# Linear attention: the inter-chunk products load their states from copies laid out slot by slot

## The chip, the cores and the metric

One NeuronCore of a Trainium2 chip. The time is the device time of the kernel in microseconds (us), the median of three runs; a profiled execution of the same program gives the rows of the trace.

## The reference, cut to what matters

The program is two two-layer networks, one after the other, in float32. The change touches the second network alone, in whose layers one of three mixers is a gated linear attention over 512 latent and 256 context tokens, with 6 heads, keys of 32 and values of 64, in both directions:

```python
GLA_HEADS, GLA_DK, GLA_DV, GLA_CHUNK = 6, 32, 64, 16

def gla_chunked(q, k, v, g, s0):
    ...
    b = jnp.cumsum(g, axis=2)
    b_last = b[:, :, -1:]
    q_dec = q * jnp.exp(b)
    k_inv = k * jnp.exp(-b)
    k_end = k * jnp.exp(b_last - b)
    ...
    a = jnp.einsum('bnihk,bnjhk->bnhij', q_dec, k_inv)
    a = jnp.where(causal, a, 0.0)
    o_intra = jnp.einsum('bnhij,bnjhv->bnihv', a, v)

    def step(s, xs):
        qd, ke, vv, dec = xs
        o = jnp.einsum('bihk,bhkv->bihv', qd, s)
        s = s * dec[..., None] + jnp.einsum('bjhk,bjhv->bhkv', ke, vv)
        return s, o
    ...
    s_final, o_inter = lax.scan(step, s0, xs)
    o = o_intra + jnp.moveaxis(o_inter, 0, 1)
```

Each chunk of 16 tokens takes the state left by the chunks before it (48 chunks in all: 16 of the context, 32 latent), and its output is the product within the chunk plus the decayed queries times that state. Both directions are added, normalized by head and multiplied with a gate.

## The kernel before, in words

Everything is written by hand for the five engines, with semaphores. In each of the two layers `gated_linear` first computes the decays and then calls `gla_group` twice, once for each group of three heads (96 partitions: 3 heads x 32 key rows). The calls are the four groups spoken of below. The first layer puts out all six token tiles of 128 (`upd` = 6), the second layer only the four latent ones (`upd` = 4).

In a group, TensorE makes each tile's state updates (L3111) and transposed scores (L3102); ScalarE, and VectorE for a sixth of them, place the updates in the tile `states`, `ST[partition, direction, 64 value columns, 49 slots]`: for each value column the 49 slots lie side by side, so that a chunk's state, 64 values, is read with a step of 49 words. VectorE masks the scores into `scoresT`. Then VectorE turns updates into states with four scans (L3190), each along the slots of all its rows: two for each direction, over 24 and over 40 of the 64 value columns, with decays that ScalarE has widened (L3216). Beside them TensorE runs the products within the chunks (L3122, scores x values, all six or four tiles), which read the scores, and then the inter-chunk products (L3128): for each tile and chunk the stationary operand is the chunk's state, 96 x 64, the moving one the chunk's queries, 96 x 48. All tiles of the first direction come first, behind the second scan; then the second direction, behind the fourth scan, tile by tile, each tile followed by the transposes (L3138) of the one before. A float32 product is two passes on TensorE, each with its own weight load.

Behind the products ScalarE copies a tile out (L3249), TensorE turns it, VectorE and ScalarE normalize it and VectorE multiplies it with the gate; the gate's activation (L3231) is ScalarE's, its multiplication with a gain (L3090) GpSimd's. In the first group of a layer TensorE at the end also turns the queries and keys of the next group (L3155). Before all this GpSimd has widened values (L3059) and copied queries (L3066).

Of the kernel before, what the change touches and what calls it, by code (L numbers as in the profile page):

```python
# [46 lines left out]
GLA_H, GLA_DK, GLA_DV, GLA_LR, CHUNK, GLA_TAU = 6, 32, 64, 16, 16, 16.0  # L47
QK = GLA_H * GLA_DK
GV = GLA_H * GLA_DV
NCH = (T + TC) // CHUNK  # L50
# [72 lines left out]
class ModulationEnd:  # L123
# [26 lines left out]
    def copy(self, dve, turned, out):  # L150
        dve.wait_ge(turned, 1)
        dve.tensor_copy(self.rows, self.bank).then_inc(out, 1)
# [13 lines left out]
class Program:  # L166
# [2841 lines left out]
    def gla_group(self, layer, grp, UG, UR, KE, DEC, MX, ON, QB, QT, KT, gain, ms, eps_t, upd, slot, SL, following):  # L3008
# [8 lines left out]
        NC8, W3, N = P // CHUNK, HG * GLA_DK, NTT * HG  # L3017
# [3 lines left out]
        V = lambda t, hh: UG[:, t, 2 * QK + (grp * HG + hh) * GLA_DV:2 * QK + (grp * HG + hh + 1) * GLA_DV]  # L3021
        with ExitStack() as ctx:
            ST = self.sbuf(ctx, "states", [W3, 2, GLA_DV, SL])
# [3 lines left out]
                sem(n) for n in ("updates", "up_out_v", "up_out_a", "zeroed", "blocked", "scanned", "scored", "masked",  # L3027
                                 "mixed", "out_done", "turned", "rows_done"))
            widened, blocked_back = sem("widened"), sem("blocked_back")
            spare = MX[:, 0:3, :].rearrange("p k n -> p (k n)")  # L3030
            VX = spare[:, 0:VR * NC8 * GLA_DV].rearrange("p (r c v) -> p r c v", r=VR, v=GLA_DV)
            parts = [(0, 24), (24, GLA_DV)]
            DX = [self.sbuf(ctx, "decay_wide", [W3, 24, SL])[:, :, :],
                  spare[0:W3, 0:(GLA_DV - 24) * SL].rearrange("p (v s) -> p v s", s=SL)]
            AT = self.sbuf(ctx, "scoresT", [P, upd, HG, 2, P])
            OT = spare[0:GLA_DV, 0:2 * HG * P].rearrange("p (r h n) -> p r h n", r=2, h=HG)
            SQ = spare[:, 2 * HG * P:2 * HG * P + 2 * W].rearrange("p (r n) -> p r n", r=2)
            own = slice(grp * W, (grp + 1) * W)
# [24 lines left out]
            def block_q(copy, d, hh):  # L3063

                r = slice(hh * GLA_DK, (hh + 1) * GLA_DK)
                return copy(QB[r, d, :, hh, :], QT[r, d, :].rearrange("p (c n) -> p c n", n=CHUNK))  # L3066

            def place(copy, n, d):

                t, hh = n // HG, n % HG  # L3070
                s0 = slot(d, t * NC8) + 1
                r = slice(hh * GLA_DK, (hh + 1) * GLA_DK)
                dst = ST[r, 0, :, s0:s0 + NC8] if d == 0 else ST[r, 1, :, s0 - NC8 + 1:s0 + 1][:, :, ::-1]
                return copy(dst, UB(n)[d * GLA_DK:(d + 1) * GLA_DK].rearrange("p (c v) -> p v c", v=GLA_DV))

            with nc.Block() as block:
                @block.gpsimd
                def _(pool):
                    for t in range(NTT):
                        for n in range(t * HG, (t + 1) * HG):  # L3080
                            if from_pool(n):
                                expand(pool, n)
                        if t % 2 == 1:
                            pool.wait_ge(expanded[0], expands((t + 1) * HG - 2))
                            block_q(pool.tensor_copy, 0, t // 2).then_inc(blocked, 1)
                            pool.wait_ge(blocked, t // 2 + 1)
                    pool.wait_ge(gate_silu, 1)
                    rows = UR[:, 0:upd, own].rearrange("p t (h v) -> p t h v", v=GLA_DV)
                    for t in range(upd):
                        pool.tensor_tensor(rows[:, t], rows[:, t], gain[:, :].unsqueeze(1).broadcast_to(  # L3090
                            [P, HG, GLA_DV]), ALU.mult).then_inc(gate_ready, 1)

                @block.tensor
                def _(pe):
# [24 lines left out]
                    for t in range(upd):  # L3119
                        for hh in range(HG):  # L3120
                            for d in range(2):
                                pe.matmul(OB(t)[:, hh, :], V(t, hh), AT[:, t, hh, d, :],  # L3122
                                          start=(hh == 0 and d == 0), stop=False, skip_group_check=True)
                    pe.wait_ge(blocked, HG)

                    def inter(t, d):
                        for c in range(NC8):
                            ins_ = pe.matmul(OB(t)[:, :, c * CHUNK:(c + 1) * CHUNK], ST[:, d, :, slot(d, t * NC8 + c)],  # L3128
                                             QB[:, d, t * NC8 + c], start=False, stop=(d == 1 and c == NC8 - 1),
                                             skip_group_check=True)  # L3130
                        return ins_
# [7 lines left out]
                                                ident[0:GLA_DV, 0:GLA_DV])  # L3139
                        ins_.then_inc(turned, 1)  # L3140

                    pe.wait_ge(scanned, 2)
                    for t in range(upd):
                        inter(t, 0)
                    pe.wait_ge(scanned, 4)
                    pe.wait_ge(blocked_back, HG)
                    for t in range(upd):
                        inter(t, 1).then_inc(mixed, 1)
# [64 lines left out]
                def _(act):  # L3213
                    def widen(k):
                        a, b = parts[k % 2]
                        act.copy(DX[k % 2], DEC[:, k // 2, grp, :].unsqueeze(1).broadcast_to([W3, b - a, SL])).then_inc(  # L3216
                            widened, 1)
# [10 lines left out]
                    for k in (2, 3):  # L3228
                        act.wait_ge(scanned, k - 1)
                        widen(k)  # L3230
                    act.activation(UR[:, 0:upd, own], UR[:, 0:upd, own], ACT.Silu).then_inc(gate_silu, 1)  # L3231

                    def square(t):
                        act.wait_ge(rows_done, t + 1)
# [325 lines left out]
```

## Time and profile before

| | |
|---|---|
| median of 3 runs | 3917.28 us (3915.54 to 3919.32) |
| profiled execution | 3916.27 us |
| its span | 3914.5 us |
| mean granted TensorE clock | 0.918 |
| TensorE busy | 3387.8 us (87%) |
| VectorE busy | 2694.3 us (69%) |
| ScalarE busy | 2125.3 us (54%) |
| GpSimd busy | 572.5 us (15%) |

The four groups stand at about 2147 to 2214, 2214 to 2277, 3312 to 3368 and 3368 to 3423 us of the span, with a granted TensorE clock of 0.76, 0.74, 0.74 and 0.75. Times in rows count from the span's start; PE is TensorE's matmul, PEld its weight load, DVE VectorE, ACT ScalarE, POOL GpSimd. PEclk is the granted clock as a share of 2.4 GHz.

### The profile page before, as it was taken

The page shows a single profiled execution, that of the slowest core. Times are in us where ns is not written, and L with a number is a line of the kernel's source. Part 1 is how long each engine was busy: PE and PEld are TensorE (multiplying, and loading weights), DVE is VectorE, ACT ScalarE, POOL GpSimd, SP SyncE. Part 2 cuts the span into 40 slices and gives each one's busy share as a digit, 9 for nine tenths or more (in the row PEclk, how much of TensorE's full clock was granted, in tenths as well). Part 3 has the DMA queues.
Part 4 walks back from the last instruction along what each step waited for, and adds up shares of the span by engine and source line. Part 5 has one row for each costly group of instructions (what it writes and reads, how often), then busy time and mean ns, then how long its engine had stood idle before and what let it go on. Part 6 is the DMA issues. An engine that isn't in the chain of part 4 may idle for free. (4 is left out here: it accounts for less than half of the span.)

```text
span 3914.5 us, 50754 instructions
## 1 busy us (share of the span) xinstructions
PE 3387.8 (87%) x17144; PEld 2769.9 (71%) x17144; DVE 2694.3 (69%) x3836; ACT 2125.3 (54%) x2780; POOL 572.5 (15%) x286
## 2 busy tenths in 40 slices
PE   8869999957978999948888987999997888879997
PEld 6757777746766777737777676888776777568875
DVE  3669999966668999976865656774565555555545
ACT  3539999943538999953444623332234445634433
POOL 0005333410004334420020300000000011300000
PEclk9879999978979999978989888999998989789998
DMA  3149999942048999953320032331331210022222
GB/s 111 49 152 396 419 418 410 407 180 94 12 164 356 419 416 416 412 200 117 104 70 2 1 108 100 117 117 65 113 105 50 58 61 1 3 80 96 93 84 81
DMA packets 148091, 651.33 MB, mean 166 GB/s; under 512 B 23478, under 2 KB 36968, under 8 KB 89448
## 3 DMA queue, kind: packets, MB, share of 16 engines
q1 hardware_dynamic: 137576, 631.59, 42.6%
q0 software_dynamic: 10080, 16.80, 1.1%
q8 instruction: 84, 1.38, 0.1%
q10 hardware_dynamic: 288, 1.05, 0.1%
q14 instruction: 63, 0.52, 0.0%
HBM read 645.01 MB, written 24.26 MB: 171 GB/s over the span
## 5 line engine op out<-in xcount | busy, mean ns | idle before, releaser
L1762 DVE TENSOR_TENSOR w_low<-w_raw,w_high 128x2048 fp32r<-128x2048 f32 x392 | 881.9, 2282 | 55.5 <-ACT w_high L1759 51.2
L1759 ACT CAST w_high<-w_raw 128x2048 fp32r<-128x2048 f32 x392 | 746.1, 1910 | 77.5 <-DMA w_raw<-in_moe_gate_dram 33.8
L2069 PE MATMUL banks<-w_high,x_split 128*128 128x512 f32 x1024 | 421.0, 411 | 46.6 <-DVE w_low L1762 39.1
L2069 PE MATMUL banks<-w_low,x_split 128*128 128x512 f32 x1024 | 407.8, 398 | 0.0
L529 PE MATMUL banks<-w_high,x_high 128*128 128x512 f32 (+2 forms) x808 | 309.6, 383 | 57.4 <-DVE w_low L435 31.5
L399 ACT CAST w_high<-w_raw 128x512 fp32r<-128x512 f32 (+2 forms) x200 | 117.8, 589 | 427.1 <-PE banks L529 421.2
L3376 PE MATMUL banks<-x_high,w_high 128*128 128x512 f32 (+1 forms) x1056 | 320.9, 358 | 21.2 <-DVE w_low L3414 21.2
L3376 PE MATMUL banks<-x_high,w_low 128*128 128x512 f32 (+1 forms) x1056 | 324.0, 361 | 0.0
L3376 PE MATMUL banks<-x_low,w_high 128*128 128x512 f32 (+1 forms) x1056 | 320.1, 357 | 0.0
L529 PE MATMUL banks<-w_high,x_low 128*128 128x512 f32 (+2 forms) x808 | 300.3, 372 | 0.0
L529 PE MATMUL banks<-w_low,x_high 128*128 128x512 f32 (+2 forms) x808 | 300.3, 372 | 0.0
L2069 PEld LDWEIGHTS banks<-w_high,x_split 128*128 128x128 f32 x1024 | 193.9, 189 | 126.4 <-DVE w_low L1762 81.9
L2019 POOL DMA_INDIRECT expert_rows<-ys,sidx x34 | 258.9, 7615 | 120.5 <-ACT ys L2239 119.6
L3399 ACT ACTIVATE convolved<-banks,taps 128x768 f32<-128x768 f32 (+1 forms) x88 | 78.0, 886 | 312.4 <-PE banks L3376 312.3
L785 PE MATMUL banks<-w_high,x_high 128*128 128x512 f32 (+2 forms) x516 | 207.4, 402 | 35.8 <-DVE w_low L753 18.9
L529 PEld LDWEIGHTS banks<-w_high,x_high 128*128 128x128 f32 x808 | 154.1, 191 | 102.0 <-DVE w_low L435 49.6
L2069 PEld LDWEIGHTS banks<-w_low,x_split 128*128 128x128 f32 x1024 | 194.2, 190 | 41.0
L3376 PEld LDWEIGHTS banks<-x_high,w_high 128*128 128x128 f32 x1056 | 176.3, 189 | 54.4 <-issue 21.8
L785 PE MATMUL banks<-w_low,x_high 128*128 128x512 f32 (+2 forms) x516 | 202.3, 392 | 0.0
L785 PE MATMUL banks<-w_high,x_low 128*128 128x512 f32 (+2 forms) x516 | 202.2, 392 | 0.0
L433 DVE TENSOR_TENSOR x_low<-mixT,x_high 128x768 fp32r<-128x768 f32 x112 | 107.3, 958 | 136.2 <-ACT x_high L400 135.7
L3376 PEld LDWEIGHTS banks<-x_high,w_low 128*128 128x128 f32 x1056 | 175.1, 189 | 30.7
(410 smaller groups left out, 7241.4 us busy)
## 6 DMA issues: line engine op xcount, KB each, us to landing
w_raw<-in_moe_gate_dram SPq DMA_DIRECT2D x132, 1024.0 KB, 10.5
w_raw<-in_moe_up_dram SPq DMA_DIRECT2D x132, 1024.0 KB, 10.2
w_raw<-in_moe_down_dram SPq DMA_DIRECT2D x132, 1024.0 KB, 10.9
w_raw<-in_ffn_w_up_dram SPq DMA_DIRECT2D x44, 1024.0 KB, 4.9
w_raw<-in_ffn_w_down_dram SPq DMA_DIRECT2D x88, 256.0 KB, 2.7
modulation<-in_w_adaT_dram SPq DMA_DIRECT2D x42, 512.0 KB, 4.2
hiddenT<-in_w_adaT_dram SPq DMA_DIRECT2D x28, 512.0 KB, 3.7
w_raw<-in_w_cols_dram SPq DMA_DIRECT2D x48, 256.0 KB, 2.9
```

Of the source, the lines that this page charges most:

```text
L399: act.copy(WS[0][:, rest % S, 0:w], W[:, rest, 0:w])
L433: dve.tensor_tensor(XS[1][:, rest % S, :], x_tile(k), XS[0][:, rest % S, :].bitcast(F32), ALU.subtract)
L529: ins_ = pe.matmul(psum_of(g), st[:, rest % S, a:b], mv[:, rest % S, x:y], start=start and first + second == 0, stop=stop and first == 1)
L785: ins_ = pe.matmul(psum_of(g), XS[first][:, k, t * P:(t + 1) * P], WS[second][:, u % S, 0:w], start=(i == 0 and first + second == 0), stop ...
L1759: act.copy(ex["WS"][0][:, v % HIGH, :], ex["WR"][:, v % RAW, :]).then_inc(ex["high"], 1)
L1762: dve.tensor_tensor(ex["WS"][1][:, v % LOW, :], ex["WR"][:, v % RAW, :], ex["WS"][0][:, v % HIGH, :].bitcast(F32), ALU.subtract).then_inc( ...
L2019: pool.indirect_dma_start(out=Y, out_offset=bass.IndirectOffsetOnAxis(ap=sidx[:, 0:1], axis=0), in_=YS[:, :], in_offset=None, bounds_check ...
L2069: ins_ = pe.matmul(GU[b][m], stationary(b, kk), WS[w][:, s, k * BANK:(k + 1) * BANK], start=(kk == 0 and w == 0), stop=(kk == KD - 1 and w ...
L3376: ins_ = pe.matmul(U(b, ab)[:, x:y], WS[first][b][:, at:at + P], XS[second][:, k, x:y], start=(k == 0 and first + second == 0), stop=(k == ...
L3399: act.activation(Z[:, ab, :], U(b, ab)[:, 0:ntok], ACT.Identity, bias=cv[:, bass.ds(f * 8 + (4 * ab + 3), 1)], scale=cv[:, bass.ds(f * 8 + ...
```

## The change

The scanned states are copied so that a slot's 64 values lie side by side, and L3128's successor loads the copies. The first direction's copy is put over the scores, whose place is free once the products within the chunks are through, and the second direction's over the rows of `states` that held the first direction. GpSimd copies value columns 0 to 24 and 48 to 64 of each direction, ScalarE columns 24 to 48. New semaphores order this: `within` is raised by the last product within the chunks, `slotted_by_pool` by each of GpSimd's four copies and `slotted_by_act` by ScalarE's two. TensorE waits for two and one of them ahead of the first direction, for four and two ahead of the second, in place of the scans.

```diff
+            within, slotted_p, slotted_a = sem("within"), sem("slotted_by_pool"), sem("slotted_by_act")
...
+            by_slot = [x[:, 0:NCH * GLA_DV].rearrange("p (s v) -> p s v", v=GLA_DV) for x in (
+                AT[0:W3].rearrange("p t h d n -> p (t h d n)"), ST[:, 0].rearrange("p v s -> p (v s)"))]
+            own_rows, late_rows = (24, 48), [(0, 24), (48, GLA_DV)]
...
+            def by_slots(copy, d, rows):
+
+                a, b = rows
+                return copy(by_slot[d][:, :, a:b], ST[:, d, a:b, 0:NCH].rearrange("p v s -> p s v"))
...
+                    pool.wait_ge(within, 1)
+                    for k in range(4):
+                        pool.wait_ge(scanned, k + 1)
+                        if k == 2:
+                            pool.wait_ge(slotted_a, 1)
+                        by_slots(pool.tensor_copy, k // 2, late_rows[k % 2]).then_inc(slotted_p, 1)
+                        pool.wait_ge(slotted_p, k + 1)
                     pool.wait_ge(gate_silu, 1)
...
-                                pe.matmul(OB(t)[:, hh, :], V(t, hh), AT[:, t, hh, d, :],
-                                          start=(hh == 0 and d == 0), stop=False, skip_group_check=True)
+                                ins_ = pe.matmul(OB(t)[:, hh, :], V(t, hh), AT[:, t, hh, d, :],
+                                                 start=(hh == 0 and d == 0), stop=False, skip_group_check=True)
+                    ins_.then_inc(within, 1)
...
-                            ins_ = pe.matmul(OB(t)[:, :, c * CHUNK:(c + 1) * CHUNK], ST[:, d, :, slot(d, t * NC8 + c)],
+                            ins_ = pe.matmul(OB(t)[:, :, c * CHUNK:(c + 1) * CHUNK], by_slot[d][:, slot(d, t * NC8 + c)],
...
-                    pe.wait_ge(scanned, 2)
+                    pe.wait_ge(slotted_p, 2)
+                    pe.wait_ge(slotted_a, 1)
                     for t in range(upd):
                         inter(t, 0)
-                    pe.wait_ge(scanned, 4)
+                    pe.wait_ge(slotted_p, 4)
+                    pe.wait_ge(slotted_a, 2)
...
+                    act.wait_ge(within, 1)
+                    by_slots(act.copy, 0, own_rows).then_inc(slotted_a, 1)
                     act.activation(UR[:, 0:upd, own], UR[:, 0:upd, own], ACT.Silu).then_inc(gate_silu, 1)
+                    act.wait_ge(scanned, 4)
+                    act.wait_ge(slotted_p, 2)
+                    act.wait_ge(slotted_a, 1)
+                    by_slots(act.copy, 1, own_rows).then_inc(slotted_a, 1)
```

GpSimd's queue in the first layer's first group, from its last copy of queries to the group's end, before (`u_r` is the gate, `q_blocks` the blocked queries):

```order
L3059 TENSOR_TENSOR mixT<-u_gla,consts 128x512 x4
L3066 COPY q_blocks<-q_decT 32x48x16
L3090 TENSOR_TENSOR u_r<-u_r,gain 128x192 x6
L3076 UNCONDITIONAL_BRANCH
L183 ISA
```

and now:

```order
L3063 TENSOR_TENSOR mixT<-u_gla,consts 128x512 x4
L3070 COPY q_blocks<-q_decT 32x48x16
L3075 COPY scoresT<-states 96x48x24
L3075 COPY scoresT<-states 96x48x16
L3075 COPY states<-states 96x48x24
L3075 COPY states<-states 96x48x16
L3106 TENSOR_TENSOR u_r<-u_r,gain 128x192 x6
```

Four copies now stand between the queries and the gate. On TensorE, at the same place, the products within the chunks and the first ones behind them, before (the last dimensions, 3x16, are a chunk's 48 query columns):

```order
L3122 MATMUL banks<-scoresT,u_gla 64x128 x36
L3128 MATMUL banks<-q_blocks,states 64x3x16 x64
L3138 MATMUL banks<-consts,mixT 128x64 x3
L3128 MATMUL banks<-q_blocks,states 64x3x16 x8
L3138 MATMUL banks<-consts,mixT 128x64 x3
```

and now:

```order
L3138 MATMUL banks<-scoresT,u_gla 64x128 x36
L3145 MATMUL banks<-q_blocks,scoresT 64x3x16 x48
L3145 MATMUL banks<-q_blocks,states 64x3x16 x16
L3155 MATMUL banks<-consts,mixT 128x64 x3
L3145 MATMUL banks<-q_blocks,states 64x3x16 x8
```

The number and the order of TensorE's products are as before; the first 48 read what now lies in the scores' place, the rest the slots over the first direction's rows. ScalarE gets one copy ahead of the gate's activation and one behind it.

## Rows read from the trace of the kernel before

**Rows 1.** Timeline of the first group: start, us, engine, line, operation, names, shapes, count.
```profile
2173.28 8.05 PE L3122 MATMUL banks<-scoresT,u_gla 128*64 128x128 f32 x72 [1.24 <-DVE scoresT L3181]
...
2175.81 4.21 DVE L3190 TENSOR_TENSOR_SCAN states<-mixT,states 96x1960 f32<-96x1960 f32 x1
...
2179.94 2.58 DVE L3190 TENSOR_TENSOR_SCAN states<-decay_wide,states 96x1176 f32<-96x1176 f32 x1
...
2181.16 14.40 PE L3128 MATMUL banks<-q_blocks,states 96*64 96x48 f32 x128
...
2182.44 4.21 DVE L3190 TENSOR_TENSOR_SCAN states<-mixT,states 96x1960 f32<-96x1960 f32 x1
...
2184.51 5.28 POOL L3090 TENSOR_TENSOR u_r<-u_r,gain 128x192 f32<-128x192 f32 x6 [14.88 <-ACT u_r L3231]
```

**Rows 2.** L3128 alone in two stretches: us, PE, PEld busy (count), PEclk, DMA.
```profile
2181.50:2185.00 3.50, 3.50 (x34) 3.50 (x33) 1.00 0.02 5
2186.00:2193.00 7.00, 7.00 (x65) 7.00 (x65) 0.50 0.00 0
```

**Rows 3.** Two stretches: PE, PEld, DVE, ACT, POOL busy (count), PEclk, DMA.
```profile
2185.40:2209.00 23.60, 23.60 (x185) 21.97 (x185) 8.26 (x24) 6.71 (x16) 4.38 (x6) 0.50 0.00 1
2209.40:2212.00 2.60, 1.26 (x12) 1.00 (x10) 2.06 (x7) 2.50 (x10) 0.00 (x0) 1.00 0.00 0
```

**Rows 4.** L1463 (a product elsewhere) alone in two stretches, columns as in rows 2.
```profile
246.50:249.90 3.40, 3.40 (x32) 3.40 (x32) 1.00 0.02 5
250.30:256.60 6.30, 6.30 (x31) 6.30 (x31) 0.50 0.00 0
```

**Rows 5.** Timeline of TensorE in the same two stretches.
```profile
246.44 3.76 PE L1463 MATMUL banks<-ring,hT 128*128 128x36 f32 x32 [1.02 <-ACT hT L1288]
...
250.01 6.81 PE L1463 MATMUL banks<-ring,hT 128*128 128x36 f32 x31
```

**Rows 6.** Timeline of the third and the fourth group: scans and products.
```profile
3339.76 4.21 DVE L3190 TENSOR_TENSOR_SCAN states<-mixT,states 96x1960 f32<-96x1960 f32 x1
...
3343.90 2.58 DVE L3190 TENSOR_TENSOR_SCAN states<-decay_wide,states 96x1176 f32<-96x1176 f32 x1
...
3344.12 10.91 PE L3128 MATMUL banks<-q_blocks,states 96*64 96x48 f32 x96 [1.57 <-DVE states L3190]
...
3399.28 2.58 DVE L3190 TENSOR_TENSOR_SCAN states<-decay_wide,states 96x1176 f32<-96x1176 f32 x1
...
3399.50 10.92 PE L3128 MATMUL banks<-q_blocks,states 96*64 96x48 f32 x96
```

**Rows 7.** L3090: timeline of the first one, and all 20 (ns min/median/max).
```profile
2184.51 2.53 POOL L3090 TENSOR_TENSOR u_r<-u_r,gain 128x192 f32<-128x192 f32 x1 [14.88 <-ACT u_r L3231]
...
L3090 POOL TENSOR_TENSOR u_r<-u_r,gain x20: 581/586/2851, 2184.5 to 3407.4; 128x192 f32<-128x192 f32 x20
```

**Rows 8.** Timeline of GpSimd and VectorE at two places ahead of the products.
```profile
2161.26 0.92 DVE L3059 TENSOR_TENSOR mixT<-u_gla,consts 128x512 f32<-128x512 f32 x1 [0.81 <-PE banks L3111]
2161.70 1.16 POOL L3066 COPY q_blocks<-q_decT 32x768 f32<-32x768 f32 x1
...
2218.91 1.04 POOL L3059 TENSOR_TENSOR mixT<-u_gla,consts 128x512 f32<-128x512 f32 x1 [0.67 <-PE banks L3111]
...
2220.01 0.81 POOL L3066 COPY q_blocks<-q_decT 32x768 f32<-32x768 f32 x1
...
2220.12 1.25 DVE L3059 TENSOR_TENSOR mixT<-u_gla,consts 128x512 f32<-128x512 f32 x1 [2.29 <-PE banks L3111]
```

**Rows 9.** Durations by line: ns min/median/max, first and last start, shapes.
```profile
L3128 PE MATMUL banks<-q_blocks,states x640: 208/311/348, 2181.2 to 3415.0; 96*64 96x48 f32 x160
...
L1463 PE MATMUL banks<-ring,hT x128: 271/279/409, 246.4 to 1153.2; 128*128 128x36 f32 x128
...
L3066 POOL COPY q_blocks<-q_decT x12: 599/951/1163, 2153.7 to 3388.0; 32x768 f32<-32x768 f32 x6, 32x512 f32<-32x512 f32 x6
...
L3216 ACT COPY decay_wide<-decay x8: 1174/1178/1181, 2147.8 to 3396.1; 96x1176 f32<-96x1176 f32 x8
```

## The prediction

> **What bounds the stage now.** I read the timeline of the linear attention's four groups first, since the change touches nothing else: two head groups in the first layer (products for six token tiles), two in the second (four tiles). In the first group [rows 1] TensorE is the bound from the score products on: L3122 starts as soon as the scores are masked and ends at 2181.33 (2173.28 + 8.05), the inter-chunk products of L3128 follow at 2181.16 without a gap, and TensorE then has no pause that an engine elsewhere explains until the group's end. VectorE's four scans run back to back beside it: the second, with which the first direction is complete, ends at 2180.02, before TensorE gets there; the fourth ends at 2186.65, while the first direction's products still run. So the scans cost nothing today. The third group differs a little: there L3122 is through early and TensorE waits 1.57 us for its second scan [rows 6].
>
> A product of L3128 is two passes, each with a weight load of 64 columns and 48 moving columns. 128 passes take 14.40 us, the last of them 0.31: 111 ns from start to start [rows 1, 9]. That is the price at both clock levels: 34 passes in 3.50 us at a granted 1.00 (2.4 GHz), 65 in 7.00 us at 0.50 (1.2 GHz) [rows 2]. A pass that does not care about TensorE's clock is held by the reading of its weights, which lie 49 words apart in the states' rows. The products spend most of their time at the low level: the clock falls at 2185.4, after some 4 us of these thin products, and stays at 0.50 for 23.6 us, until the 128-column transposes of the group's end [rows 3].
>
> **The weight load, slot by slot.** After the change the 64 columns lie side by side. The nearest rows for that are L1463's: 128 columns side by side, 36 moving columns, so the load bounds them too. Less the last one's own 0.28 and 0.41 us, 32 passes take 3.76 us, 112 ns from start to start, at 1.00, and 31 passes 6.81 us, 213 ns, at 0.50 [rows 4, 5, 9]. This load does follow the clock. Half the columns make 56 ns at the high level and 107 ns at the low one. The gain per pass is therefore 55 ns at 1.00 and 4 ns at 0.50, and all of it for 640 passes is 35.2 us or 2.6 us. Everything turns on the clock during the products.
>
> **The new wait.** The first direction's copies go into the scores' place, so none can start before L3122 is through. ScalarE copies a third of it; GpSimd two parts, one after the other, of 24 and 16 rows (1152 and 768 elements for a partition). TensorE now waits for both. VectorE's scans are running at just that time, and the rows show what GpSimd does beside VectorE. The first multiplication of L3090 takes 2.53 us when it falls into the fourth scan, its kind 0.586 [rows 7]: subtracting, it began in effect at 2186.45, 0.20 us before the scan's recorded end of 2186.65. It holds for a copy as well: L3066's copy takes 1.16 us when a two-input operation of VectorE is running, 0.81 when none is, and in that last row VectorE is the one that waits: its 0.92 us become 1.25, so that it began 0.37 us before GpSimd's recorded end [rows 8]. The two take turns, whole instruction by whole instruction.
>
> The Trainium skill says the same more widely (SBUF — State Buffer, Who interferes with whom): VectorE and GpSimd share a pair of SBUF ports as an exclusive lock, held for the whole instruction, also against a VectorE operation with two SBUF inputs. The scans are of that kind, so by this rule every copy during them waits; were it not so, the time would be the last rival's below.
>
> So in the first group: the third scan ends at 2182.52 and GpSimd's copy of a us runs from 2182.32. The fourth scan has been queued since 2182.44, while GpSimd must first see its own semaphore, so I let the scan go next: from 2181.95 + a, for 4.21 less the 0.08 by which scans overlap in the record, to 2186.08 + a. The second copy, of b us, runs from 2185.88 + a, and with 0.15 us for the semaphore (the same as between the third group's second scan, which ends at 3343.97, and its first product at 3344.12 [rows 6]) TensorE starts at 2186.03 + a + b instead of 2181.16: later by 4.87 + a + b. The second group repeats these rows one for one, so it has the same. The same working gives 5.87 + a + b for the fourth (its third scan ends at 3401.86, its products start at 3399.50 [rows 6]), and 1.73 + a + b for the third, where the first copy goes behind the second scan and only the short third scan (2.58 us) lies between the copies.
>
> Price of a and b: no row shows a GpSimd copy that reads at this stride. From below, L3066's copies, 0.81 us for 768 elements and 0.60 for 512 [rows 8, 9], make 0.83 ns for an element: a = 1.13, b = 0.81. From above, L3059's 1.04 us for 512 elements, 2.0 ns for each [rows 8]: a = 2.3, b = 1.55. The copy is nearest to L3066; the stride doubled a weight load (111 against 56 ns), and I put half of that on it: a = 1.6, b = 1.1. The waits then are 7.57, 7.57, 4.43 and 8.57 us, together 28.1 us, between 25.1 and 32.7.
>
> **The clock after that.** TensorE stands still for 7 us where it now works, and then runs products of the same 48 columns every 107 ns, hardly denser than those that stay at 0.50 for 23.6 us now. The clock fell after thinner work and rose only with wide transposes. I take 0.50 for all 640 passes: 2.6 us saved.
>
> The Trainium skill gives a rule without the clock (TensorE: Matmul & The Clock Gate, LDWEIGHTS): a load takes its columns over 1.2 ns, here 53 ns at either level. By it all passes would cost about 56 and save 35.2 us, 3912 in the second rival below; but 128 columns took 213 ns at 0.50, not 107, so the measurement decides against it.
>
> **The rest costs nothing.** ScalarE's first copy (1.17 us for 1176 elements side by side [rows 9], twice that at worst) lies beside GpSimd's; it pushes the gate's activation back, for which only GpSimd's multiplications wait, and the second copy is done some 1.5 to 3 us after the fourth scan, near 2190. GpSimd's two copies for the second direction end near 2191.6 in the first group, and its six multiplications 3.5 us later. All this lies beside the first direction's products (48 products, 96 passes, 10.3 us from 2188.7; in the third group 6.9 us to 3355.4, the copies being ready at 3355.0). If this cover went, the third group would lose up to 2.8 us, as the rivals count. The scans' lateness of some 1.2 us matters to nobody: VectorE's next work is a tile's rows, after the second direction's first products. Nothing is queued behind TensorE's new wait but its own products. The transfers are untouched.
>
> **Sum.** 28.1 - 2.6 = +25.5 us on the profiled execution's own 3916.27 us (span 3914.5): 3941.8. The runs' median lies 1.0 higher, so 3942 stands between. Its own range: 25.1 - 2.6 to 32.7, that is 3938 to 3950; it also holds the case that the change doesn't make loads any quicker (28.1, 3944).
>
> **Rivals.**
> 1. GpSimd's second copy slips in behind the first, before the fourth scan. For it: the copies are adjacent in its queue. Against: the scan already waits for the port, GpSimd for a semaphore. The starts then slip by 4.2, 4.2, 2.7 and 5.2 us, 16.2 in all, and the third group's second direction, whose copies now wait behind the fourth scan, costs 2 us: +15.6, 3932.
> 2. The clock is high during the products. For it: at 1.00, passes of 56 ns are twice as dense as now, so once high it may stay. Against: it must rise first, after a pause, from 107 ns passes. At 1.00 throughout: 28.1 - 35.2 + 2.8 (the third group's second direction then waits for GpSimd's fourth copy) = -4.3, 3912. If it rises after the first 64 passes of each group, 4 x 64 x 51 ns = 13 us are lost again: 3924. I price it at 3918.
> 3. Faster: the scans do not hold the copies. Then TensorE waits only for a + b and three semaphores after L3122: 3.3, 3.3, 1.6 and 3.2 us. With the clock kept, 11.4 - 35.2 + 3.9 (third and fourth group waiting for the fourth scan and ScalarE's copy) = -19.9: 3896. It decides where the pause stays so short that the clock holds; with the low clock it is 11.4 - 2.6, 3925. For it: no row has a copy beside a scan. Against: [rows 7, 8].
>
> **Chances.** The forecast 0.69 (with the loads that don't gain), rival 1 0.08, rival 2 0.13, rival 3 0.06, dearer copies beyond 3950 0.04. A change of under 0.2% (7.8 us) is about what a measurement of this kernel can't tell from none: 3909.4 to 3925.1. Faster by more: rival 3 with its clock and a little of rival 2, 0.07. Within: rival 2, 0.14. Slower: 0.79. The range 3920 to 3950 holds the forecast, rival 1 and the upper third of rival 2.
>
> **What would show it.** Right: a pause of TensorE of 4 to 9 us ahead of the first inter-chunk product in each group; in GpSimd's first copy about 1 us of waiting and in its second some 4 us, ending just behind the fourth scan (the third in the third group); that scan recorded a good 1 us longer; passes of 107 ns at 0.50. Wrong: passes near 56 ns with a granted 1.00, copies that end inside a scan, or a pause under 4 us in the six-tile groups.

## The result, and the profile after

The changed kernel takes 3950.26 us (median of six runs, 3937.55 to 3954.91), the kernel before 3917.57 us beside it: a ratio of 1.0084, 95% interval 1.0070 to 1.0098. The change costs 32.7 us. The profiled execution took 3949.64 us with a span of 3947.9; its mean granted TensorE clock was 0.913, against 0.918 before.

This is the first group in the timeline after the change (start, us, engine, line; L3138 are the products within the chunks, L3145 the inter-chunk ones, L3209 the scans, L3075 the new copies, L3106 the multiplications with the gain).

```profile
2172.38 8.05 PE L3138 MATMUL banks<-scoresT,u_gla 128*64 128x128 f32 x72 [1.24 <-DVE scoresT L3200]
...
2179.04 2.58 DVE L3209 TENSOR_TENSOR_SCAN states<-decay_wide,states 96x1176 f32<-96x1176 f32 x1
...
2180.55 8.47 POOL L3075 COPY scoresT<-states 96x1152 f32<-96x1152 f32 x2 [11.82 <-PE banks L3138]
2180.89 2.26 ACT L3075 COPY scoresT<-states 96x1152 f32<-96x1152 f32 x1
2181.54 6.21 DVE L3209 TENSOR_TENSOR_SCAN states<-mixT,states 96x1960 f32<-96x1960 f32 x1
...
2189.08 3.79 POOL L3075 COPY states<-states 96x1152 f32<-96x1152 f32 x2
...
2189.10 2.25 ACT L3075 COPY states<-states 96x1152 f32<-96x1152 f32 x1 [3.47 <-issue]
2189.12 10.45 PE L3145 MATMUL banks<-q_blocks,scoresT 96*64 96x48 f32 x96 [8.70 <-POOL scoresT L3075]
2192.96 3.33 POOL L3106 TENSOR_TENSOR u_r<-u_r,gain 128x192 f32<-128x192 f32 x6
```

In [rows 1] the inter-chunk products followed the products within the chunks without a gap. Now TensorE waits 8.70 us, and the timeline names GpSimd's copy as what it waited for. GpSimd's two copies take 8.47 us while the scans run and 3.79 us, with the same shapes, when they don't. The fourth scan is recorded 2.00 us longer than before (6.21 against 4.21). ScalarE's copy takes 2.26 us beside a scan and 2.25 without one: nothing holds it.

The copies one by one, from the line's own view in the stretch of the first direction and in that of the second (ns min/median/max; with two instructions these are the shorter and the longer).

```profile
L3075 POOL COPY scoresT<-states x2: 3106/4206/5307, 2180.5 to 2183.7; 96x1152 f32<-96x1152 f32 x1, 96x768 f32<-96x768 f32 x1
...
L3075 POOL COPY states<-states x2: 1492/1866/2239, 2189.1 to 2191.4; 96x1152 f32<-96x1152 f32 x1, 96x768 f32<-96x768 f32 x1
```

Undisturbed the copies cost a = 2.24 and b = 1.49 us. In the first direction they are recorded with 3.11 and 5.31: the first waits about 0.87 us for the third scan to end, the second about 3.82 us for the fourth.

The stretches of the first group (busy time of PE, PEld, DVE, ACT, POOL, then PEclk), to be read beside [rows 2, 3]:

```profile
2180.40:2184.40 4.00, 0.03 (x1) 0.00 (x0) 4.00 (x2) 3.98 (x3) 3.79 (x2) 0.99 0.00 0
2184.40:2189.10 4.70, 0.00 (x0) 0.01 (x1) 3.36 (x1) 1.22 (x2) 4.64 (x2) 0.50 0.00 0
2189.10:2212.20 23.10, 23.08 (x204) 22.27 (x204) 3.99 (x13) 7.80 (x14) 7.04 (x8) 0.50 0.01 1
```

TensorE's clock falls to 0.50 in the pause, and all inter-chunk products run at that level. The 96 passes of the first direction take 10.45 us, 107 ns from start to start.

In the kernel before, the products within the chunks took 5.42 us in the third group and 7.09 in the fourth:

```profile
3337.13 5.42 PE L3122 MATMUL banks<-scoresT,u_gla 128*64 128x128 f32 x48 [2.42 <-issue]
...
3392.50 7.09 PE L3122 MATMUL banks<-scoresT,u_gla 128*64 128x128 f32 x48 [2.42 <-issue]
```

Now they take 7.09 us in the third group as well:

```profile
3354.41 7.09 PE L3138 MATMUL banks<-scoresT,u_gla 128*64 128x128 f32 x48 [2.41 <-issue]
...
3361.17 2.58 DVE L3209 TENSOR_TENSOR_SCAN states<-decay_wide,states 96x1176 f32<-96x1176 f32 x1
...
3361.62 9.53 POOL L3075 COPY scoresT<-states 96x1152 f32<-96x1152 f32 x2 [10.78 <-PE banks L3138]
```

The window over the third group's products has a mean granted clock of 0.76:

```profile
3354.40:3361.40 7.00, 6.99 (x48) 6.85 (x48) 6.88 (x3) 4.80 (x6) 0.00 (x0) 0.76 0.01 2
```

So the first copy comes 0.45 us after the third scan has begun, and the first inter-chunk product starts 16.74 us after the group's first scan, as in the other three groups.

### The profile page after: what moved, and what is told of

It reads as the page before. It is cut to its first block and busy times, and to the rows that moved or that the text cites. A ratio compares the mean times of both kernels' runs of the same rounds, so it can differ in the third digit from the quotient of the medians.

```text
span 3947.9 us, 50798 instructions
## 1 busy us (share of the span) xinstructions
PE 3387.1 (86%) x17144; PEld 2770.1 (70%) x17144; DVE 2700.6 (68%) x3836; ACT 2141.6 (54%) x2788; POOL 638.5 (16%) x302
## 5 line engine op out<-in xcount | busy, mean ns | idle before, releaser
L3401 PEld LDWEIGHTS banks<-x_low,w_high 128*128 128x128 f32 x1056 | 174.5, 189 | 30.7
## 6 DMA issues: line engine op xcount, KB each, us to landing
w_raw<-in_moe_gate_dram SPq DMA_DIRECT2D x132, 1024.0 KB, 10.5
```

Source lines behind the costliest of these rows:

```text
L3401: ins_ = pe.matmul(U(b, ab)[:, x:y], WS[first][b][:, at:at + P], XS[second][:, k, x:y], start=(k == 0 and first + second == 0), stop=(k == ...
```

## The experiments

The timeline gives a measure of the stage: the start of the first and of the last inter-chunk pass, counted from the start of the group's first scan. The third column adds up what the last pass has moved in all four groups against the kernel before. Stretches outside the stage differ by some us from run to run (the first group's first scan starts between 2172.0 and 2176.7 us), so medians and stage agree within 4 us only. The measure ends with the last pass: in no_copies, whose last pass in the first group comes 10.5 us earlier, the second group's first scan comes 8.2 us sooner.

| kernel | first / last pass, us: first group; third; fourth | stage, sum | median, us | ratio, 95% interval |
|---|---|---|---|---|
| before | 7.88 / 31.80; 6.88 / 22.41; 6.88 / 22.41 | 0 | 3917.6 to 3918.2 | |
| changed | 16.74 / 39.81; 16.74 / 31.64; 16.74 / 31.64 | +34.5 | 3950.26 | 1.0084 (1.0070 to 1.0098) |
| hold_fourth | 12.92 / 35.99; 12.91 / 29.64; 12.62 / 29.35 | +22.6 | 3944.78 | 1.0065 (1.0052 to 1.0078) |
| one_copy | 12.69 / 35.76; 12.69 / 28.52; 12.68 / 28.52 | +20.1 | 3937.44 | 1.0055 (1.0042 to 1.0068) |
| turned_loops | 16.49 / 39.56; 16.49 / 31.39; 16.49 / 31.39 | +33.5 | 3948.08 | 1.0078 (1.0066 to 1.0091) |
| plain_copies | 14.99 / 38.07; 14.98 / 29.88; 10.85 / 25.75 | +23.3 | 3938.65 | 1.0056 (1.0043 to 1.0070) |
| no_copies | 7.88 / 21.26; 6.88 / 21.52; 6.88 / 21.52 | -22.9 | 3895.68 | 0.9943 (0.9931 to 0.9956) |
| filled | 12.66 / 28.69; 13.80 / 25.82; 12.66 / 25.08 | -0.5 | 3918.07 | 1.0002 (0.9993 to 1.0011) |
| second_only | 7.87 / 31.33; 6.88 / 25.09; 6.88 / 25.10 | +4.4 | 3925.07 | 1.0016 (1.0007 to 1.0025) |
| early | 8.48 / 28.16; 6.88 / 22.41; 6.88 / 22.41 | -7.3 | 3907.73 | 0.9978 (0.9969 to 0.9987) |
| early_filled | 8.50 / 24.52; 6.88 / 22.38; 6.88 / 22.39 | -14.4 | 3906.49 | 0.9975 (0.9965 to 0.9984) |

The second group repeats the first within 0.05 us, but for the last pass of filled (28.29) and early_filled (24.78).

### hold_fourth: is it the scans that hold the copies?

```diff
                         dve.wait_ge(widened, k + 1)
+                        if k == 3:
+                            dve.wait_ge(slotted_p, 2)
```

> The changed kernel, with one wait more: VectorE's fourth scan starts only when GpSimd has made both of its first-direction copies. My theory (GpSimd's copies and VectorE's scans take turns, so the second copy is held behind the whole fourth scan): the second copy follows the first at once and takes about 1.5 us; TensorE's pause ahead of the first inter-chunk product falls from 8.7 and 9.8 us to about 4.9 and 6.0; in the two four-tile groups the late fourth scan and the copies behind it cost about 1.3 us each ahead of the second direction; 3950 - 15 + 2.6 = about 3938. Rival (the copies are slow by themselves, the scans don't hold them): the second copy still takes about 5 us, and the pause stays or grows: 3950 or more.

The timeline of its first group, and of the copies and scans of its fourth:

```profile
2184.55 4.66 POOL L3075 COPY scoresT<-states 96x1152 f32<-96x1152 f32 x2 [11.82 <-PE banks L3138]
...
2189.28 2.21 POOL L3075 COPY states<-states 96x1152 f32<-96x1152 f32 x1
...
2189.32 10.45 PE L3145 MATMUL banks<-q_blocks,scoresT 96*64 96x48 f32 x96 [4.88 <-POOL scoresT L3075]
2189.32 6.28 DVE L3211 TENSOR_TENSOR_SCAN states<-mixT,states 96x1960 f32<-96x1960 f32 x1 [3.69 <-POOL scoresT L3075]
...
3417.40 5.43 PE L3138 MATMUL banks<-scoresT,u_gla 128*64 128x128 f32 x48 [2.42 <-issue]
...
3422.95 7.08 POOL L3075 COPY scoresT<-states 96x1152 f32<-96x1152 f32 x2 [9.11 <-PE banks L3138]
3424.17 4.58 DVE L3211 TENSOR_TENSOR_SCAN states<-decay_wide,states 96x1176 f32<-96x1176 f32 x1
```

With the scan out of the way both copies together take 4.66 us instead of 8.47, and the pause is 4.88 us, as expected (4.9): the turns are shown. What I had not expected is the next turn: GpSimd, now free, starts its third copy (2.21 us) 0.04 us ahead of the fourth scan, which is recorded 2.07 us longer for it. The late states cost the second direction of the four-tile groups 1.8 us each, not 1.3. The stage gains 11.9 us on the changed kernel, the medians 5.5 only: 3944.78 us where 3938 was expected, and the intervals of the two ratios overlap. It is the trace that shows the turn here, not the time.

The fourth group shows something else. Here the products within the chunks took 5.43 us, the first copy was ready before the second scan ended, and the third scan is the one recorded 2.00 us longer (4.58 against 2.58): the copy got in ahead of it. I come back to this below.

### one_copy: one turn instead of two

```diff
-            own_rows, late_rows = (24, 48), [(0, 24), (48, GLA_DV)]
+            own_rows, late_rows = (0, 24), (24, GLA_DV)
...
-                    for k in range(4):
-                        pool.wait_ge(scanned, k + 1)
+                    for k in range(2):
+                        pool.wait_ge(scanned, 2 * k + 2)
...
```

> The changed kernel, with GpSimd's two copies of a direction made into one: rows 24 to 64 in one instruction once both scans of that direction are done; ScalarE copies rows 0 to 24. My theory (each separate copy loses a turn to a scan): one copy of 1920 elements takes about 3.7 us once it has its turn, and loses only the turn to the third scan: pause of about 4.9 us in the six-tile groups and 6.0 in the four-tile ones, about 3938, the same as with the fourth scan held back. Rival (the copies' elements set the time, not turns): the pause stays at 8.7 to 9.8 us, about 3950.

Timeline of its first group:

```profile
2182.52 4.42 POOL L3075 COPY scoresT<-states 96x1920 f32<-96x1920 f32 x1 [11.82 <-PE banks L3138]
...
2183.51 7.53 DVE L3209 TENSOR_TENSOR_SCAN states<-mixT,states 96x1960 f32<-96x1960 f32 x1
...
2187.04 10.44 PE L3145 MATMUL banks<-q_blocks,scoresT 96*64 96x48 f32 x96 [4.64 <-POOL scoresT L3075]
```

The same 1920 elements in one instruction are through after one turn: a pause of 4.64 us, and 3937.44 us where 3938 was expected. (In the four-tile groups of this run the products within the chunks ended early, so the pause from there is 7.4 us, while the first product still starts 12.69 us after the first scan.) The fourth scan waits 3.3 us, and nobody waits for it long: the second direction of a four-tile group starts 0.9 us late.

### turned_loops and plain_copies: what a copy costs

```diff
-                return copy(by_slot[d][:, :, a:b], ST[:, d, a:b, 0:NCH].rearrange("p v s -> p s v"))
+                return copy(by_slot[d][:, :, a:b].rearrange("p s v -> p v s"), ST[:, d, a:b, 0:NCH])
```

> The changed kernel, with the two loops inside every copy exchanged: it reads 48 slots side by side and writes them 64 words apart, the same elements to the same places. Theory that the jumping reads doubled the price: GpSimd's copies fall from 2.25 and 1.48 us to about 1.13 and 0.81, ScalarE's from 2.26 to about 1.2; the pause is 1.8 us shorter in each of the four groups, about 3943. Rival (jumping writes cost the same as jumping reads, or the price goes by element whatever the order): 2.25 and 1.48 us again, 3950.

```diff
+                by_row = by_slot[d].rearrange("p s v -> p (s v)")[:, a * NCH:b * NCH].rearrange("p (v s) -> p v s", s=NCH)
+                return copy(by_row, ST[:, d, a:b, 0:NCH])
```

> The changed kernel, whose copies move the same rows to the same buffers without turning them: row after row, 48 words side by side on both sides. The products load the same addresses as in the changed kernel and so multiply wrongly ordered numbers. Theory that jumping by many words, on the reading or on the writing side, doubles the price of an element: GpSimd's copies fall to about 1.13 and 0.81 us, ScalarE's to about 1.2 us, the pause in each group is 1.8 us shorter, about 3943. Rival (this many elements over 96 partitions cost that much in any order): 2.25 and 1.48 us as before, 3950.

First the copies of the second direction, undisturbed, in turned_loops, from the line's view:

```profile
L3075 POOL COPY states<-states x2: 1491/1832/2173, 2189.6 to 2191.9; 96x1152 f32<-96x1152 f32 x1, 96x768 f32<-96x768 f32 x1
...
L3075 ACT COPY states<-states x1: 2173/2173/2173, 2189.7 to 2189.7; 96x1152 f32<-96x1152 f32 x1
```

The same in plain_copies:

```profile
L3076 POOL COPY states<-states x2: 822/983/1144, 2189.6 to 2190.8; 96x1152 f32<-96x1152 f32 x1, 96x768 f32<-96x768 f32 x1
...
L3076 ACT COPY states<-states x1: 1152/1152/1152, 2189.6 to 2189.6; 96x1152 f32<-96x1152 f32 x1
```

Jumping on the writing side costs as much as jumping on the reading side (2.17 and 1.49 us), so the rival of turned_loops was right; without jumps GpSimd needs 1.14 and 0.82 us, ScalarE 1.15. So a turned copy costs twice a plain one, on both engines. The first product of plain_copies starts 1.75 us earlier (14.99 against 16.74).

Its fourth group ran with early products within the chunks, as the fourth of hold_fourth, and here nothing is held back by hand:

```profile
3413.66 5.43 PE L3139 MATMUL banks<-scoresT,u_gla 128*64 128x128 f32 x48 [2.42 <-issue]
...
3419.21 5.32 POOL L3076 COPY scoresT<-states 96x1152 f32<-96x1152 f32 x2 [9.12 <-PE banks L3139]
3420.43 3.48 DVE L3210 TENSOR_TENSOR_SCAN states<-decay_wide,states 96x1176 f32<-96x1176 f32 x1
...
3423.83 4.79 DVE L3210 TENSOR_TENSOR_SCAN states<-mixT,states 96x1960 f32<-96x1960 f32 x1
```

The window over its products within the chunks:

```profile
3413.60:3419.00 5.40, 5.34 (x48) 5.21 (x48) 5.23 (x2) 4.74 (x5) 0.00 (x0) 1.00 0.02 3
```

At a clock of 1.00 TensorE was done with them after 5.43 us, the first copy went behind the second scan and the second behind the third, and the first product started at 10.85 instead of 14.98 us: 4.1 us less, for nothing but the order of the turns. That is why plain_copies came to 3938.65 where 3943 was expected.

### no_copies: what the contiguous loads are worth

```diff
-                        by_slots(pool.tensor_copy, k // 2, late_rows[k % 2]).then_inc(slotted_p, 1)
...
-                    by_slots(act.copy, 0, own_rows).then_inc(slotted_a, 1)
...
-                    pe.wait_ge(slotted_p, 2)
-                    pe.wait_ge(slotted_a, 1)
+                    pe.wait_ge(scanned, 2)
...
```

> The changed kernel without the copies: the inter-chunk products load 64 words side by side out of the scans' own tile, so they multiply wrong numbers, and TensorE waits for the scans as before the change. This is what the contiguous loads are worth without the pause. My theory (a load that follows the clock, and denser passes without a pause hold the high level): passes of 56 ns at a granted 1.00; 640 x 55 ns = 35 us less, and 3 us given back in each of the four-tile groups to the fourth scan: about 3888. Rival (the clock falls for passes of 48 columns anyway): 107 ns at 0.50 for most of them, about 3915.

Stretches of the first and of the third group:

```profile
2183.40:2197.00 13.60, 13.23 (x207) 12.62 (x204) 8.03 (x10) 7.70 (x13) 5.27 (x6) 1.00 0.01 2
3338.50:3346.80 8.30, 8.26 (x70) 7.83 (x70) 0.97 (x3) 3.05 (x6) 2.01 (x4) 0.50 0.01 2
```

In the six-tile groups, where the products follow without a pause, the clock stays at 1.00 to their end: the first direction's 96 passes start within 5.52 us, 58 ns apart, and the last pass comes 10.5 us earlier. In the four-tile groups, which start with the wait of 1.57 us that stands in [rows 6] too and wait again for the fourth scan, it falls to 0.50, and 0.9 us is all that is gained. Both theories were right, each in one kind of group, which gives 3896, between their 3888 and 3915.

### filled: is it the pause that takes the clock?

```diff
+                    def fill(n):
+                        for _ in range(n):
+                            pe.matmul(self.ps[0:GLA_DV, 7, 0:P], ident[:, 0:GLA_DV], masks[:, 0, :], start=True, stop=True)
...
+                    fill(20 if upd == NTT else 32)
                     pe.wait_ge(slotted_p, 1)
                     pe.wait_ge(slotted_a, 1)
...
+                    fill(9 if upd == NTT else 17)
                     pe.wait_ge(slotted_p, 2)
...
```

> The version with one GpSimd copy per direction, whose TensorE pauses are filled with products of constants of 128 moving columns into a spare bank (20 and 9 of them in the six-tile groups, 32 and 17 in the four-tile ones, ahead of the first and of the second direction). They are extra work whose results nobody reads. My theory (the pause is what drops TensorE's clock, and with it goes the worth of the contiguous loads): TensorE stays at a granted 1.00, passes take 57 to 60 ns as without copies, the last inter-chunk product comes about 7.5 us earlier in the six-tile groups and 3 us earlier in the four-tile ones than with one copy: 3937 - 20 = about 3917. Rival (the clock falls for other reasons, the pause has no part in it): passes of 107 ns, 3937 or a little more.

The filling (L3145) and the first direction (L3149) in the first group's timeline:

```profile
2179.89 4.53 PE L3145 MATMUL banks<-consts 128*64 128x128 f32 x40
...
2184.68 5.80 PE L3149 MATMUL banks<-q_blocks,scoresT 96*64 96x48 f32 x96 [0.26 <-POOL scoresT L3075]
```

Stretches of the first direction and of the start of the second, first group:

```profile
2184.60:2190.50 5.90, 5.82 (x98) 5.83 (x99) 4.12 (x1) 2.40 (x2) 1.68 (x2) 1.00 0.00 0
2192.40:2199.00 6.60, 6.29 (x90) 5.74 (x89) 1.26 (x5) 4.08 (x8) 3.35 (x7) 1.00 0.00 0
```

The copies, the turns and the late start are those of one_copy (first product at 12.66 us), but with TensorE kept busy the clock stays at 1.00, in the first group until 0.9 us ahead of the last pass, and the passes take 59 ns. That alone is worth 19.4 us: 3918.07 against 3937.44, with 3917 expected. (In the third group, whose products within the chunks took 7.09 us, the filling ends later than the copies, and the first product starts at 13.80.) With the clock kept, this version costs nothing against the kernel before.

### second_only: the half that is hidden

```diff
-                    for k in range(4):
+                    for k in range(2, 4):
...
-                    by_slots(act.copy, 0, own_rows).then_inc(slotted_a, 1)
...
-                            ins_ = pe.matmul(OB(t)[:, :, c * CHUNK:(c + 1) * CHUNK], by_slot[d][:, slot(d, t * NC8 + c)],
+                            ins_ = pe.matmul(OB(t)[:, :, c * CHUNK:(c + 1) * CHUNK], (by_slot[1][:, slot(d, t * NC8 + c)] if d else ST[:, 0, :, slot(d, t * NC8 + c)]),
...
```

> Half of the change: only the second direction's states are copied (into the scores' place), the first direction's products load the scanned rows as before the change. My theory (the loss is the wait ahead of the first direction; copies that lie beside its products cost nothing, and at the low clock the contiguous loads give back 4 ns a pass): no pause ahead of the first product, nothing lost in the six-tile groups, a wait of about 3 us ahead of the second direction in each four-tile group, where only 7 us of products cover the fourth scan and the copies: 3918 - 2 + 6 = about 3922. Rival (the copies cost wherever they are, by slowing scans, products or gate work): about half of the change's 33 us or more, 3934 and up.

The first group's timeline:

```profile
2183.23 10.83 PE L3143 MATMUL banks<-q_blocks,states 96*64 96x48 f32 x96
...
2184.75 7.61 POOL L3075 COPY scoresT<-states 96x1152 f32<-96x1152 f32 x2 [13.05 <-DVE states L3206]
```

Again GpSimd's copy sits behind the fourth scan, now for 3.8 us, and in the six-tile groups nobody minds: the last pass is 0.5 us earlier than before the change. In the four-tile groups the second direction starts 3.0 us later, as expected. By the stage this makes +4.4 us; the median is 7.4 us up. Most of the change's loss, 30 of 34.5 us by the stage and 25 of 32.7 by the medians, is the first direction's.

### early and early_filled: the copies where they fit

The first layer only; the second is as before the change. The place of the queries and keys is free from the first scan on, so the copies need not wait for the products within the chunks, and ScalarE and VectorE make them.

```diff
+                        by_slots(act.copy, 0, (0, 24)).then_inc(slotted_a, 1)
+                        act.wait_ge(scanned, 2)
+                        by_slots(act.copy, 0, (24, 40)).then_inc(slotted_a, 1)
+                        widen(3)
...
+                            by_slots(dve.tensor_copy, d, (40, GLA_DV)).then_inc(slotted_v, 1)
...
+                        pe.wait_ge(slotted_v, 1)
+                        pe.wait_ge(slotted_a, 2)
...
```

> First layer only (the second layer's groups are as before the change): the copies of the first direction go into the place of the decayed queries and keys, which is free before the within-chunk products end, and are made by ScalarE (rows 0 to 40, the first 24 while the second scan runs) and VectorE (rows 40 to 64, between its second and third scan); GpSimd builds the second direction's query blocks instead of ScalarE. My theory (the loss is the wait and the clock that falls in it): TensorE's pause ahead of the first inter-chunk product is under 1 us, the clock holds through the first direction, 57 ns a pass; the second direction waits some 2.5 us for the later scans and their copies. If the clock holds through that as well, the last product comes 7 to 8 us earlier than before the change in each of the two groups, about 3903; if it falls there, 2 us earlier, about 3913. Rival (a strided copy on VectorE costs several us, or copies and scans disturb each other on these engines too): a pause of 3 us or more, the clock falls, 3920 to 3930.

> The early copies, with 12 products of constants on TensorE ahead of the second direction, whose results nobody reads. My theory (a pause drops the clock): if the plain early version loses its clock between the directions, this one keeps it, with passes of 57 to 60 ns to the end: about 3903. Rival (the clock falls during the thin passes themselves, whatever stands between them): the same time as the plain early version.

The timeline of early's first group:

```profile
2183.48 1.57 ACT L3076 COPY qk_turned<-states 96x768 f32<-96x768 f32 x1 [0.78 <-DVE states L3212]
2183.48 1.20 DVE L3076 COPY qk_turned<-states 96x1152 f32<-96x1152 f32 x1
...
2185.19 5.77 PE L3142 MATMUL banks<-q_blocks,qk_turned 96*64 96x48 f32 x96 [0.44 <-ACT qk_turned L3076]
```

Two of its stretches, the first direction and the start of the second:

```profile
2185.20:2191.00 5.80, 5.76 (x96) 5.64 (x96) 5.80 (x2) 5.77 (x4) 1.60 (x1) 1.00 0.01 3
2193.00:2199.00 6.00, 6.00 (x59) 5.59 (x60) 0.78 (x3) 1.80 (x5) 2.40 (x5) 0.60 0.01 3
```

The two directions in early_filled:

```profile
2180.70:2186.50 5.80, 5.80 (x98) 5.80 (x99) 5.80 (x2) 5.77 (x4) 1.60 (x1) 1.00 0.01 3
2188.90:2196.90 8.00, 7.63 (x110) 6.99 (x108) 2.48 (x8) 4.50 (x10) 2.02 (x4) 1.00 0.01 2
```

The pause ahead of the first direction is 0.44 us and the clock holds. Ahead of the second direction TensorE waits 2.03 us, and the clock falls behind that wait in early, not in early_filled: the last pass comes 3.6 us earlier than before the change in the one, 7.3 in the other. Both kernels are faster than either of the two compared: 0.9978 and 0.9975. Expected were about 3903 where the clock holds to the end and 3913 where it falls between the directions. The two profiled executions took 3901.58 (early_filled) and 3911.67 (early), but the medians lie between, 3906.49 and 3907.73: that early_filled beats early, as the stage says by 7 us, they do not confirm. The mean granted clocks of the executions overlap, 0.920 to 0.923 and 0.918 to 0.921, so the two traces show what the filling does in one execution each, not how often early loses its clock.

## Why the prediction was right, and where it was wrong

It said 3942 with a range up to 3950, and slower; it is slower, and at 3950.26 just past the range. By its own steps:

- **TensorE's new wait, its place and its cause**: right. The pause stands ahead of the first inter-chunk product in each group, and GpSimd's second copy ends behind the fourth scan (in the third group too, where the third was predicted; see below). That copies and scans take turns by whole instructions is shown by hold_fourth and one_copy, which remove a turn each and move the first product by 3.8 and 4.1 us in a six-tile group. The Trainium skill's rule (SBUF — State Buffer, Who interferes with whom), an exclusive lock held for the whole instruction, agrees; it also says that ScalarE waits for nobody, as its 2.26 us beside a scan against 2.25 show.
- **The clock and the passes**: right. 0.50 for all inter-chunk products, 107 ns a pass; the time from the first to the last pass fell from 23.92 to 23.07 and from 15.53 to 14.90 us, 2.96 us in all against the 2.6 predicted. The high level's price, 56 ns, was measured as 58 to 59 (no_copies, filled). Rival 2 needed the clock high: its passes came, 59 ns at 1.00, only where the pause is filled, short or absent (filled, early, the six-tile groups of no_copies).
- **The hidden work**: right. The second direction follows the first without a pause in the changed kernel.
- **The step that failed: the size of the delays**, 28.1 us predicted and 37.4 measured (8.86 us in each six-tile group, 9.86 in each four-tile one). Three terms make up the 9.3 us.
  1. The price of a and b. The prediction put half of the stride's doubling on L3066's price, 1.6 and 1.1 us; the doubling was whole, 2.24 and 1.49 (plain_copies gives 1.14 and 0.82 without it, which is the prediction's lower bound). That is 1.03 us in each group, 4.1 us.
  2. The order of turns in the third group. The prediction let its first copy go behind the second scan, which the run before allowed, with its products within the chunks through in 5.42 us; in the profiled run after they ran at a mean clock of 0.76, took 7.09 us and ended behind the third scan's start, and the group lost the turn: 4.1 us. What the prediction took for a property of the third group differs from execution to execution: early, whose second layer works as in the kernel before, has 7.09 us in the third group and 5.43 in the fourth. The mechanism as predicted does occur, when the products end early: hold_fourth's fourth group has its first product 5.74 us later than before where the prediction's 1.73 + a + b gives 5.46 with the measured a and b, and plain_copies shows both orders in one run.
  3. The hand-over. The fourth scan began 0.11 us ahead of the copy's recorded end, not 0.37, and took its whole 4.21 us, not 4.13; the second copy and TensorE followed 0.07 us sooner than reckoned. Net, that is 0.26 us in each group, 1.0 us.
- **The sum**: 37.43 - 2.96 = +34.47 us in the stage; the profiled executions differ by 33.4, the medians by 32.7. Only the profiled execution shows its turns, and which turns the other five had is not shown. With the price alone set right the prediction would have been 3946, with the third group as well 3950.

The range was too narrow on the upper side: it held the dear copies or the third group's lost turn, not both.

What stays open: why the products within the chunks of a four-tile group run at 1.00 in some executions and at a mean 0.76 in others. In all 22 four-tile groups of the eleven traces TensorE stands still for 2.41 to 2.43 us ahead of them. In 10 groups the granted clock is then 0.50 for a part of these products, and they take 7.09 us; in 12 it is 1.00 throughout, and they take 5.42 or 5.43. No run here shows what decides it.

## What to carry to other kernels

Before a copy is added to straighten a stride, see which engine is free to make it: here GpSimd's copies and VectorE's two-input scans took turns by whole instructions, and each turn saved, by one copy in place of two or by holding the scan back, brought the first product some 4 us forward. The only versions that gained had the copies on ScalarE and VectorE, where they fit. Price a pause of TensorE with what its clock does afterwards: here the contiguous loads gave back 3 us after the pause and 23 us without it. When an order of turns hangs on who is first by a fraction of a us, put both orders into the range, and don't take the order that one trace shows for a property of the program.

## What the runs showed of the hardware that was not expected

- A copy that jumps by 64 or 49 words on one side costs twice a plain one: GpSimd 2.24 against 1.14 us for 1152 elements, ScalarE 2.25 against 1.15. VectorE made the same jumping copy of 1152 elements in 1.20 us (1.40 in the second direction, with GpSimd's multiplications beside it). The Trainium skill (GPSIMD Engine Reference, Performance pitfalls for Q7 kernels) puts reads with a large step at half as much again for an element; here it is 1.96 times, and the measurement decides.
- Products of 48 moving columns ran at a clock of 1.00 for 13.6 us in no_copies, with no pause ahead of them and 58 ns apart in the first direction; behind the pause of the changed kernel the same products ran at 0.50, every 107 ns.
